# First projections on x without its norm, zero rows written later, a reciprocal in pieces, and ScalarE's branch ahead of its last eviction, in a hybrid two-layer kernel

## The reference

```python
def rms_norm(x, w):
    y = x * lax.rsqrt(jnp.mean(x * x, axis=-1, keepdims=True) + RMS_EPS)
    return y * w

def even_layer(x, ...):
    xn = rms_norm(x, norm_mix)
    p = xn @ w_in                          # 1024 x 2816
    lru_x, lru_gate, p_rw = p[..., :512], p[..., 512:1024], p[..., 1024:]
    y_lru = rg_lru(causal_dwconv(lru_x, ...), ...) * gelu(lru_gate)
    y_rw = rwkv7_mix(p_rw, ...)            # p = p + mu * (token_shift(p) - p), then
                                           # LoRAs, a state recurrence in chunks of 64
    x = x + concatenate([y_lru, y_rw]) @ w_out
    return x + swiglu(rms_norm(x, norm_ffn), ffn_w1, ffn_w3, ffn_w2)

def odd_layer(x, ...):                     # mLSTM, then top-2 of 8 experts
    ...
    return x + moe_swiglu(rms_norm(x, norm_ffn), router, moe_w1, moe_w3, moe_w2)

return rms_norm(odd_layer(even_layer(x)), final_norm)
```

## Time and profile before

| | |
|---|---|
| median of 3 runs | 1255.91 us (1255.16 to 1258.74) |
| profiled execution | 1256.21 us, its span 1254.3 us |
| PE busy | 1223.6 us (98%), 12721 matmuls |
| DVE, ACT, POOL busy | 279.9, 164.9, 53.3 us |
| mean granted TensorE clock | 0.995 |
| DMA | 359.52 MB, mean 287 GB/s |

### The profile page before, as it was taken

The page is one execution under the profiler, slowest core; times in us unless marked ns, Lnnn a source line. Parts: engine busy times, 40 slices in busy tenths (PEclk is TensorE's granted clock), DMA queues, the critical chain, the costliest instruction groups (busy, mean ns, idle before and its releaser), DMA issues.

```text
span 1254.3 us, 27155 instructions
## 1 busy us (share of the span) xinstructions
PE 1223.6 (98%) x12721; PEld 980.1 (78%) x12721; DVE 279.9 (22%) x618; ACT 164.9 (13%) x346; POOL 53.3 (4%) x58
## 2 busy tenths in 40 slices
PE   6999999999999999999999999999999999999997
PEld 5888978888888889874467777778777777777773
DVE  2657554000000375442011101110111011001104
ACT  3415311000000125340000000000000000000001
POOL 0014000000000000000000000000000000000000
PEclk9999999999999999999999999999999999999999
DMA  9601077345100826449999999999999999999954
GB/s 356 245 1 68 4 261 292 134 172 197 52 1 1 328 68 273 197 190 396 398 420 416 417 416 415 414 419 418 410 419 419 414 417 413 413 416 412 390 188 187
DMA packets 76872, 359.52 MB, mean 287 GB/s; under 512 B 6504, under 2 KB 14064, under 8 KB 60112
## 3 DMA queue, kind: packets, MB, share of 16 engines
q1 hardware_dynamic: 73216, 347.25, 69.4%
q0 software_dynamic: 3232, 10.36, 2.2%
q10 hardware_dynamic: 304, 0.10, 0.1%
HBM read 350.72 MB, written 6.96 MB: 285 GB/s over the span
## 4 chain that ended last, share of the span: by engine, by line
PE 96%; DVE 2%; ACT 1%; issue 1%; DMA 1%; DVEq 0%; SPq 0%
PE ps L593 95%; DMA cf<-in_cf 1%; DVE W L1633 0%; ACT S L1293 0%; DVE S L1630 0%; DVE W L1632 0%; DVE xn L2016 0%; PE ps L978 0%; ACT S L1483 0%; DVE rs L1515 0%; DVE W L1666 0%; DVE W L1668 0%; ACT L1480 0%; ACT L1293 0%; DVE S L1860 0%
## 5 line engine op out<-in xcount | busy, mean ns | idle before, releaser
L593 PE MATMUL ps<-W,S 128*32 128x352 f32 (+3 forms) x9008 | 699.6, 467 | 2.0 <-DVE W L1949 0.9
L593 PEld LDWEIGHTS ps<-W,S 128*32 128x32 f32 (+1 forms) x9008 | 523.8, 111 | 176.6 <-issue 28.1
L593 PE MATMUL ps<-xn,W 128*128 128x256 f32 (+1 forms) x1456 | 321.6, 380 | 3.0 <-DVE xn L1522 3.0
L593 PEld LDWEIGHTS ps<-xn,W 128*128 128x128 f32 (+1 forms) x1456 | 275.0, 190 | 44.9 <-issue 6.7
L1959 DVE TENSOR_TENSOR S<-S,ps 128x352 f32<-128x352 f32 x48 | 25.0, 521 | 590.5 <-ACT S L1431 587.2
L593 PE MATMUL ps<-S,W 128*128 128x256 f32 (+2 forms) x584 | 123.8, 366 | 0.0
L593 PEld LDWEIGHTS ps<-S,W 128*128 128x128 f32 (+2 forms) x584 | 103.1, 185 | 14.5 <-issue 1.1
L1431 ACT ACTIVATE S<-ps 128x352 f32<-128x352 f32 x48 | 20.5, 462 | 604.9 <-PE ps L593 601.2
L593 PE MATMUL ps<-W 64*64 64x64 f32 (+1 forms) x1296 | 51.1, 228 | 5.6 <-issue 2.4
L593 PEld LDWEIGHTS ps<-W 64*64 64x64 f32 (+1 forms) x1296 | 48.2, 141 | 7.7 <-issue 4.0
L1730 DVE TENSOR_TENSOR S<-S,ps 128x256 f32<-128x256 f32 x20 | 8.4, 421 | 194.6 <-ACT S L1341 194.6
(11 more groups left out here) (273 smaller groups left out, 429.1 us busy)
## 6 DMA issues: line engine op xcount, KB each, us to landing
W<-in_moe SPq DMA_DIRECT2D x128, 1408.0 KB
W<-in_moe SPq DMA_DIRECT2D x176, 512.0 KB
W<-in_l_ffn_w SPq DMA_DIRECT2D x12, 2048.0 KB
W<-in_l_w_in SPq DMA_DIRECT2D x5, 2048.0 KB
W<-in_l_ffn_w SPq DMA_DIRECT2D x6, 1536.0 KB
W<-in_l_w_out SPq DMA_DIRECT2D x2, 4096.0 KB, 21.6
W<-in_l_w_in SPq DMA_DIRECT2D x2, 4096.0 KB, 15.9
y_rows<-W POOLq DMA_DIRECT2D x4, 512.0 KB, 4.4
```

Of the source, the lines that this page charges most:

```text
L593: return nc.tensor.matmul(o, l, r, start=start, stop=stop, **kw)
```

## The change

- SP loads x and the first weight block in halves of four k, alternating; the second block is split in two pairs of columns; cf without its first 130 columns (the norm's constants) comes behind the second weight block, and these first columns come on ACT's queue, behind vec.
- DVE multiplies x by the norm's weight into a new tile xwa (eight instructions) and adds ACT's squares up in pairs. PE starts project(0) on xwa, in halves of k, then takes the mean with a single product on the summed squares (summed_mean), and then project(1), also on xwa. DVE multiplies both results in PSUM by the reciprocal root (raw_scaled). xn is formed by normed behind the first shift, for project(2) and later. The small logarithm for the RG-LRU on DVE comes after the second shift.
- The zero rows are written behind y_rw 2 and up_done 6, from another place in SBUF, and SP no longer waits for them.
- The two reciprocals of 128x512 in the RG-LRU become four of 128x256: one before the first level, two in lru(1), one in lru(2).
- At the end ACT runs through its branch and loads the root's table before the last expert_out; DVE's total(0) comes before the last add_half.

```diff
-        WIN_BLOCKS = [(20, 2), (12, 4), (8, 4), (0, 4), (16, 4), (4, 4)]
+        WIN_BLOCKS = [(20, 2), (12, 2), (14, 2), (8, 4), (0, 4), (16, 4), (4, 4)]
+        xwa = S[:, 5632:5632 + KD * T].rearrange("p (k t) -> p k t", k=KD)
-        zero = W[:, RC - D:RC]
+        zero = S[:, 11584:11584 + D]
...
# SP
-            sp.dma_start(x[:, :, :], A["xT"].rearrange("(k p) t -> p k t", p=P)).then_inc(in_x, 16)
-            sp.dma_start(cf[:, :], A["cf"]).then_inc(in_con, 16)
+            for k0, got_x, got_w in ((0, in_x, in_win[0]), (4, in_x2, in_win2)):
+                sp.dma_start(x[:, k0:k0 + 4, :], xT[:, k0:k0 + 4, :]).then_inc(got_x, 16)
+                sp.dma_start(win[0][:, k0:k0 + 4, :], w[:, k0:k0 + 4, 20 * P:22 * P]).then_inc(got_w, 16)
             for b, (j0, n) in enumerate(WIN_BLOCKS):
-                sp.dma_start(win[b], w[:, :, j0 * P:(j0 + n) * P]).then_inc(in_win[b], 16)
+                if b:
+                    sp.dma_start(win[b], w[:, :, j0 * P:(j0 + n) * P]).then_inc(in_win[b], 16)
                 if b == 1:
+                    sp.dma_start(cf[:, ONES:], A["cf"][:, ONES:]).then_inc(in_late, 16)
                     sp.dma_start(small0, A["small0"]).then_inc(in_small0, 16)
...
-            sp.wait_ge(pool_io, 16 * 5)
...
# POOL
-            pool.wait_ge(proj, 11)
+            pool.wait_ge(y_rw, 2)
+            pool.wait_ge(up_done, 6)
             step(nc.gpsimd.memset(zero, 0.0))
...
# PE
-            norm_mean(0, 4)
-            project(0)
-            project(1)
+            for half_k in range(2):
+                pe.wait_ge((in_win[0], in_win2)[half_k], 16)
+                for u in range(2):
+                    for k in range(4 * half_k, 4 * half_k + 4):
+                        pe.wait_ge(xw_done, k + 1)
+                        ins = mm(ps[:, 0, u * T:(u + 1) * T], win[0][:, k, u * P:(u + 1) * P], xwa[:, k, :],
+                                 k == 0 and u == 0, k == KD - 1, skip_group_check=True)
+            ins.then_inc(proj, 1)
+            summed_mean(0, 4, xn)
+            pe.wait_ge(in_win[1], 16)
+            for u in range(2):
+                for k in range(KD):
+                    ins = mm(ps[:, 1, u * T:(u + 1) * T], win[1][:, k, u * P:(u + 1) * P], xwa[:, k, :], k == 0, k == KD - 1)
+            ins.then_inc(proj, 1)
...
# ACT
             act.dma_start(vec[:, :], A["vecs"]).then_inc(in_con, 16)
+            act.dma_start(cf[:, 0:ONES], A["cf"][:, 0:ONES]).then_inc(in_con, 16)
...
-                act.wait_ge(omm_done, 1)
+                act.wait_ge(omm_done, i + 2 if i < 2 else 1)
...
             experts(0)
             with act.If(over != 0):
...
             A_(misc[:, 86:87], con(EPS, n=1), ACT.Sqrt)
+            expert_out(0, E - 1)
...
# DVE
-            normed(0, "l0_norm_mix", xn)
+            def raw_scaled(i):
+                dve.wait_ge(proj, i + 1)
+                raw = ps[:, i, :].rearrange("p (u t) -> p u t", u=2)
+                V.tensor_tensor(raw, raw, rs[:, :].unsqueeze(1).broadcast_to([P, 2, T]), ALU.mult).then_inc(omm_done, 1)
+            for k0, got_x in ((0, in_x), (4, in_x2)):
+                dve.wait_ge(got_x, 16)
+                for k in range(k0, k0 + 4):
+                    V.tensor_scalar(xwa[:, k, :], x[:, k, :], col("l0_norm_mix", k), None, ALU.mult).then_inc(xw_done, 1)
+                for k in ((2,), (4, 6))[k0 // 4]:
+                    dve.wait_ge(sq_done, k + 2)
+                    step(V.tensor_tensor(xn[:, 0:2, :], xn[:, 0:2, :], xn[:, k:k + 2, :], ALU.add))
+            step(V.tensor_tensor(xn[:, 0, :], xn[:, 0, :], xn[:, 1, :], ALU.add), sum_done)
+            inverse_root(0)
+            raw_scaled(0)
...
             shift(0)
+            normed(0, "l0_norm_mix", xn)
+            raw_scaled(1)
             shift(1)
...
-            step(V.reciprocal(ld[:, 0:2, :], ld[:, 0:2, :]))
+            step(V.reciprocal(ld[:, 0:1, :], ld[:, 0:1, :]))
...
-                if part == 1:
-                    step(V.reciprocal(ld[:, 2:4, :], ld[:, 2:4, :]))
+                for j in {1: (1, 2), 2: (3,)}.get(part, ()):
+                    step(V.reciprocal(ld[:, j:j + 1, :], ld[:, j:j + 1, :]))
...
-            for c, i in ((0, 0), (0, 1), (1, 0), (1, 1)):
+            for c, i in ((0, 0), (0, 1), (1, 0)):
                 add_half(adds(0, E - 1), c, i, xn_done)
             total(0)
+            add_half(adds(0, E - 1), 1, 1, xn_done)
```

More of the change, by code:

```diff
@@ L292, in hybrid_rglru_rwkv7_mlstm_moe @@
         in_d = [sem(f"in_d{i}") for i in range(DSLOTS)]
-        in_win, in_small0 = in_d[0:6], in_d[6]
+        in_win = in_d[0:7]
         in_wo0 = sem("in_wo0")
@@ L299, in hybrid_rglru_rwkv7_mlstm_moe @@
         stored = sem("stored")
+        in_x2, in_win2, in_small0 = in_xm, in_z, in_wo1
         in_m, IM0 = in_con, 32
@@ L349, in hybrid_rglru_rwkv7_mlstm_moe @@
         ix_done, IX0 = sp4_done, 1
-        xg_done, XG0 = omm_done, 1
+        xg_done, XG0 = omm_done, 3
         ADDS = 4
@@ L538, in _ @@
             nc.gpsimd.memset(lxp[:, :, 0:3], 0.0).then_inc(zeroed, 1)
-            pool.wait_ge(in_con, 32)
+            pool.wait_ge(in_late, 48)
             pool.wait_ge(proj, 1)
@@ L593, in mm @@
                 return nc.tensor.matmul(o, l, r, start=start, stop=stop, **kw)
[L595 to L600, removed]
             def summed_mean(i, bank, squares):
-                pe.wait_ge(sum_done, i)
+                pe.wait_ge(sum_done, i + 1)
                 mm(ps[:, bank, 0:T], con(MEAN_D), squares[:, 0, :], True, True).then_inc(mean_done, 1)
             pe.wait_ge(in_con, 32)
-            norm_mean(0, 4)
             def drained(turn):
@@ L626, in project @@
                     for k in range(KD):
-                        if i == 0 and u == 0:
+                        if i == 2 and u == 0:
                             pe.wait_ge(xn_done, k + 1)
@@ L677, in _ @@
             pe.wait_ge(root_done, 1)
+            pe.wait_ge(in_late, 48)
             for i in range(2):
@@ L846, in up_unscaled @@
                 for k in range(KD):
-                    pe.wait_ge(xw_done, k + 1)
+                    pe.wait_ge(xw_done, KD + k + 1)
                     for a, w in enumerate((w1r, w3r)):
@@ L895, in project_unscaled @@
                 for k in range(KD):
-                    pe.wait_ge(xw_done, KD + k + 1)
+                    pe.wait_ge(xw_done, 2 * KD + k + 1)
                     for u in range(2):
@@ L900, in project_unscaled @@
                 ins.then_inc(p1, 1)
-            pe.wait_ge(in_xm, 16)
+            pe.wait_ge(in_xm, 32)
             project_unscaled(0)
@@ L914, in _ @@
                 if i == 4:
-                    pe.wait_ge(in_z, 16)
+                    pe.wait_ge(in_z, 32)
                 if i == 5:
@@ L989, in _ @@
                 weighted(h)
-            pe.wait_ge(in_wo1, 16)
+            pe.wait_ge(in_wo1, 32)
             for i in range(4):
@@ L1225, in norm_root @@
                 A_(rs[:, :], ps[:, bank, 0:T], ACT.Sqrt, bias=con(EPS, n=1)).then_inc(root_done, 1)
-            act.wait_ge(in_x, 16)
-            norm_squares(lambda k: None)
+            norm_squares(lambda k: act.wait_ge((in_x, in_x2)[k // 4], 16))
             act.wait_ge(in_con, 32)
@@ L1346, in _ @@
             act.wait_ge(gt_done, 1)
-            act.wait_ge(in_late, 32)
+            act.wait_ge(in_late, 48)
             A_(row[:, 0, :], ps[32:40, 4, 0:T], ACT.Copy)
@@ L1461, in experts @@
                         gate(n, 2 * e + 2)
-                    expert_out(n, e)
                     if e < E - 1:
+                        expert_out(n, e)
                         gate(n, 2 * e + 3)
@@ L1478, in _ @@
                 for turn in range(1, PASSES):
+                    expert_out(turn - 1, E - 1)
                     experts(turn)
+                act.wait_ge(m_d, NB * E * PASSES)
+                act.wait_ge(m_sc, adds(PASSES - 1, E - 1))
             A_(misc[:, 86:87], con(EPS, n=1), ACT.Sqrt)
+            expert_out(0, E - 1)
             for c, i in ((0, 0), (0, 1), (1, 0), (1, 1)):
@@ L1483, in _ @@
                 A_(junk[:, 2 * c + i, :], xtok[:, c, 512 * i:512 * (i + 1)], ACT.Square, accum_out=fsum[:, 2 * c + i:2 * c + i + 1]).then_inc(sq_done, 1)
-                if (c, i) in ((1, 0), (1, 1)):
-                    act.wait_ge(sum_done, 3 + i)
+                if c:
+                    act.wait_ge(sum_done, 4 + i)
                     A_(frec[:, i:i + 1], ftot[:, i:i + 1], ACT.Sqrt, scale=1.0 / D, bias=con(EPS, n=1)).then_inc(root_done, 1)
@@ L1517, in normed @@
             def normed(i, name, dst):
-                if i not in (1, 2):
+                if i > 2:
                     inverse_root(i)
@@ L1527, in _ @@
             V.tensor_scalar(OKA, vec[:, VECS["l0_k_a"]:VECS["l0_k_a"] + 4], -1.0, 1.0, ALU.mult, ALU.add)
-            dve.wait_ge(in_x, 16)
-            normed(0, "l0_norm_mix", xn)
[L1530 to L1534, removed]
+            def raw_scaled(i):
[12 more added lines that the diff above has]
```

(11 more changed lines are left out.)

1 line of the change is left out of this document (added).

## The result

The changed kernel takes 1243.8 us (median of 4 executions, 1240.19 to 1245.87) beside 1256.2 of the kernel before: a ratio of 0.9891, with a 95% interval of 0.987 to 0.9912. The forecast was 1242.5, range 1239.9 to 1247.3. On another chip the same kernel took 1245.51 beside 1257.43, ratio 0.9899 (0.9871 to 0.9928).

The account below looks back on a forecast made before the run. PE, busy 98% of the span, was taken as the bound. Gains of 7.9 + 1.2 + 4.1 + 0.25 = 13.45 us from 1256.21 gave 1242.8, median 1242.5; own range 1240.0 to 1245.0, extended to 1247.3.

Parts of the forecast that it names:

- Start: Up to the LoRA product: new load order and projections ahead of the norm gain 7.9 us, bounds 6.0 to 8.4.
- rival C: At the start, the constants' second DMA on ACT's queue starves behind SP's stream; each us past 6.5 costs one; chance 0.03.
- slow first stretch: PE's first eight products took 5.85 us, 0.73 each against 0.44 later; project(0)'s first half now pays it.
- Rival B: Start gains less, slow pace lasting longer or constants landing at 8 or later: 1247.2, likelier 1245; chance 0.14.
- Rival D: Behind the start, DVE becomes late for kk (2 us of slack), losing up to 1.5: 1244; chance 0.08.
- Reciprocal: At the inverse's first level, reciprocals in pieces end PE's wait for DVE's Z: 1.2 us, bounds 0.9 to 1.3.
- Zeros: At the inverse, moving the zero rows ends PE's 2.4 us gap and the low clock: 4.1 us, bounds 0 and 4.4.
- part 2: The reciprocals in pieces, ending PE's wait for Z at the inverse: gain 1.2 us.
- part 3: The zero rows written later, ending PE's "issue" gap and the low clock behind it: gain 4.1 us.
- New place: Zeros behind up_done 6, where PE takes few instructions: 5 to 6 us of DMA, cost 0, bounds 0 to 1.
- Tail: Behind the last expert, ACT's squares begin earlier, beside DVE's adds: gain 0.25 us, bounds 0 to 0.5.
- What shifts by chance: Low granted clock after the state chain, 0.59 over 4.2 us: up to 1.7 us less or as much more.

Follow-up runs that it names:

- the warm start: Changed kernel plus eight PE products on a zeroed tile while waiting for the first weights: 1241.92 us, ratio 0.9866; again on another chip 1241.95, ratio 0.9871.

## Why the prediction was right, point by point

- **Start: 7.9 forecast, 8.02 found.** PE began at 6.98 (7.0), project(0) took 9.45 (9.4), the LoRA product came at 23.69 (23.85). tanh had 1.4 us to spare where I had 1.7. The constants on ACT's queue were there at 5.36, where I took 6.5; rival C had nothing to it. That the slow first stretch moves to project(0) was right, and the warm start shows it. My reading of its granted clock as 1.00 was wrong: the trace has no record of the clock there, and the pace is that of the lower level. Rival B had a point in that its length isn't fixed: in the second profile of the same kernel project(0) took 0.67 us more. Rival D, DVE late behind the start, didn't happen: from the LoRA product to the first copy of level 1 it takes 86.77 us in the changed kernel and also in the kernel before with the reciprocals in pieces.
- **Reciprocal: 1.2 forecast, 1.33 found,** by the changed kernel and by undoing it.
- **Zeros: 4.1 forecast, 4.18 found, in part by luck.** The step that gave it to this part alone failed. I costed parts 2 and 3 as independent. They aren't: either alone takes the gap away (only the zeros: 5.60 between the copies; only the reciprocals: 5.67), and only with both undone does it come back (7.90). The sum came out right because both were in the change. Had only part 2 been made, my sum would have been 4 us short; had part 3 been added on top of it, 4 us too much. I also took all of the 4.1 as the price of the stall. 1.8 of them are the low clock behind it, which came in the one profile of the kernel before and not in the run with both undone; the stall alone is 2.3. The cause itself, instructions that come late behind the zeros, stood: the gap goes with the zeros to wherever PE uses instructions fastest. Where the pages of the Trainium skill speak against it, they are half right. That queues take turns by packet ("DMA: Bandwidth & Descriptors", Queues, rings and completion order) is seen in the two runs where a packet due 1.1 us into the zeros gets through 1.9 us into them; it isn't seen in the three where packets due at 2.3, 2.4 and 3.1 us started only with the end of the zeros, 3.6, 3.5 and 2.8 us late. What decides between the two I can't say.
- **New place: 0 forecast, 0 found.** From ACT's first silu out of PSUM in the feed-forward (220.29 and 208.82) to its first for the experts (585.84 and 574.42) it takes 365.55 us before and 365.60 after, with the zeros running from 242.5 to about 253 us in it, longer than the 5 to 6 us that I gave.
- **Tail: 0.25 forecast, 0.3 won behind the first add,** and lost to DVE's branch in this pair, though not in most other profiles.
- **What shifts by chance: up to 1.7 either way forecast, 2.1 lost in the profiled pair.** The forecast of 1242.8 for the profiled execution against 1244.61 is this term. It is larger than I gave: in the changed kernel alone the time from the recurrence's start to the first residual add is 44.66 us in one profile and 46.87 in another, and up to 49.5 in runs that change nothing in this stretch. That the median, 1243.8, came so near the forecast of 1242.5 has some luck in it; on the other chip it was 1245.51, still within the range.

## What to carry to other kernels

Of several edits that each remove a cause of the same stall, each looks as if it were worth the whole stall: cost them together, and undo them in pairs as well as one by one. A gap without a semaphore, in a dense stretch of small instructions and behind a large transfer, is worth a look at the instruction queue's packets; move the transfer to where the engine uses few instructions. While PE waits for its first weights, products on a zeroed tile can take over the slow first stretch; here they cost nothing.

## What the runs showed of the hardware

- A 16 KB instruction packet due 1.1 us into a stream of stores at 390 GB/s came through 0.8 us late (two runs), while three that were due 2.3 to 3.1 us into it started only with its end. PE went on for 3.5 to 3.8 us from the time the packet was due, about as long as one packet lasts it in this stage (3.7 us), and then stood still for 1.5 to 2.4 us.
- In the first microseconds of PE's work eight products take 5.2 to 6.5 us instead of 3.6. The granted clock reads 1.00 there only because the trace has no record of it yet; the records begin 3.1 to 6.0 us after PE's first product, and the pace doubles there.
- The busy time of weight loads on the page was 980.1 us in the profile of before and 756 to 765 us in all others, also where the number of loads is the same (12721; 757.8 with only the zeros moved); the time doesn't go with it, so this is the record, not the kernel.
